# Moving the start addresses of TensorE's operands in SBUF, in a fused two-block transformer kernel

## The reference

```python
# block 1
h    = rmsnorm(x, g_attn)
proj = h @ w_in                       # 2048 x 6144, and 8 forget-gate columns
mixed = concat(head_rmsnorm(stick_breaking(q, k, v)), head_rmsnorm(forgetting(q, k, v, log_f)))
x    = x + mixed @ w_out              # 2048 x 2048
u    = relu(rmsnorm(x, g_mlp) @ w_up) # 2048 x 8192
x    = rmsnorm(x + (u * u) @ w_down, g_final)
# block 2
proj = rmsnorm(x) @ w_in_2            # 2048 x 7168, and 16 narrow columns
x    = x + concat(hgrn2(...), gated_delta(...)) @ w_out_2
x    = x + peer(rmsnorm(x))           # 16384 experts: all up products, top-16 gates, all down products
return rmsnorm(x, final_norm_g_2)
```

## Time and profile before

| | |
|---|---|
| time, median of 2 runs | 3211.09 us (3210.66 to 3211.52) |
| span of the profiled execution, first to last instruction | 3209.0 us |
| time less span | 2.1 us |
| mean granted TensorE clock | 0.999 |
| TensorE busy | 3191.6 us, 99% of the span, 19975 matmuls |
| VectorE, ScalarE, GpSimd busy | 2030.1, 1447.3, 496.9 us |
| DMA | 644.18 MB, mean 201 GB/s |

### The profile page before, as it was taken

How to read it: one execution, slowest core, us unless ns; L and a number is a source line. 1 busy time by engine, 2 the same in 40 slices (tenths; PEclk the granted TensorE clock), 3 DMA queues, 4 the chain that set the end, 5 groups by cost and what they waited for, 6 DMA issues and landing times.

```text
span 3209.0 us, 48201 instructions
## 1 busy us (share of the span) xinstructions
PE 3191.6 (99%) x19975; PEld 2854.0 (89%) x19975; DVE 2030.1 (63%) x1837; ACT 1447.3 (45%) x1271; POOL 496.9 (15%) x418
## 2 busy tenths in 40 slices
PE   9999999999999999999999999999999999999999
PEld 7888899999999888888989999999999888888887
DVE  5455665556555667765476888999975555555554
ACT  5454453333433364464444444555544433334333
POOL 0000000000000002136200002888840000000000
PEclk9999999999999999999999999999999999999999
DMA  7444565555555453342255566677676656556563
GB/s 282 165 159 158 172 225 194 196 186 193 195 187 193 158 183 119 132 158 105 93 211 204 199 216 222 224 251 251 229 263 259 241 225 261 228 230 257 226 261 118
DMA packets 129572, 644.18 MB, mean 201 GB/s; under 512 B 12672, under 2 KB 45840, under 8 KB 60304
## 3 DMA queue, kind: packets, MB, share of 16 engines
q1 hardware_dynamic: 95792, 623.03, 53.3%
q10 hardware_dynamic: 33632, 18.99, 1.9%
HBM read 606.31 MB, written 35.66 MB: 200 GB/s over the span
## 4 chain that ended last, share of the span: by engine, by line
PE 97%; DVE 1%; ACT 1%; DMA 0%; SPq 0%; issue 0%; DVEq 0%; ACTq 0%
PE pj L305 12%; PE pj L304 12%; PE pj L306 12%; PE pj L282 7%; PE pj L281 7%; PE pj L280 7%; PE pj L1774 4%; PE pj L1772 4%; PE pj L890 4%; PE pj L892 4%; PE pj L1773 4%; PE pj L891 4%; PE pm L282 2%; PE pt L282 2%; PE pt L281 2%; PE pm L281 2%
## 5 line engine op out<-in xcount | busy, mean ns | idle before, releaser
L262 ACT ACTIVATE hi<-raw 128x2048 fp32r<-128x2048 f32 x534 | 1023.8, 1917 | 1372.7 <-PE pj L306 640.7
L269 DVE TENSOR_TENSOR lo<-raw,hi 128x2048 fp32r<-128x2048 f32 x400 | 918.5, 2296 | 677.5 <-ACT hi L262 676.7
L304 PE MATMUL pj<-xh,hi 128*128 128x256 f32 x3328 | 919.9, 276 | 0.0
L305 PE MATMUL pj<-xl,hi 128*128 128x256 f32 x3328 | 918.8, 276 | 0.0
L306 PE MATMUL pj<-xh,lo 128*128 128x256 f32 x3328 | 918.8, 276 | 0.0
L305 PEld LDWEIGHTS pj<-xl,hi 128*128 128x128 f32 x3328 | 625.0, 188 | 0.6
L304 PEld LDWEIGHTS pj<-xh,hi 128*128 128x128 f32 x3328 | 624.8, 188 | 0.6
L306 PEld LDWEIGHTS pj<-xh,lo 128*128 128x128 f32 x3328 | 624.8, 188 | 0.0
L269 DVE TENSOR_TENSOR lo_in<-raw,hi 128x2048 fp32r<-128x2048 f32 x134 | 308.1, 2300 | 268.9 <-ACT hi L262 268.4
L2495 POOL TENSOR_SCALAR hotA<-cst,slotT 128x128 fp32r<-128x128 f32 x256 | 337.9, 1335 | 462.0 <-ACT slotT L2333 425.4
L1772 PE MATMUL pj<-hi,xh 128*128 128x512 f32 x576 | 232.3, 403 | 0.0
(11 more groups left out here) (408 smaller groups left out, 4243.8 us busy)
## 6 DMA issues: line engine op xcount, KB each, us to landing
raw<-w_peer SPq DMA_DIRECT2D x256, 1024.0 KB, 6.3
raw<-w_mlp SPq DMA_DIRECT2D x128, 1024.0 KB, 4.8
raw<-w_in SPq DMA_DIRECT2D x102, 1024.0 KB, 4.8
raw<-w_out SPq DMA_DIRECT2D x32, 1024.0 KB, 4.8
raw<-w_q SPq DMA_DIRECT2D x16, 1024.0 KB, 4.9
act_scratch<-hidU SPq DMA_DIRECT2D x32, 512.0 KB, 3.0
gates_scratch<-stage ACTq DMA_DIRECT2D x8, 2048.0 KB, 17.5
hidV<-act_scratch SPq DMA_DIRECT2D x32, 512.0 KB, 3.7
```

The lines of the kernel that those rows point to most:

```text
L262: nc.scalar.activation(hi[:, j, :], raw[:, j, :], ACT.Copy).then_inc(hi_ready, 1)
L269: nc.vector.tensor_tensor(low(q)[:, j, :], raw[:, j, :], hi[:, j, :].bitcast(F32), ALU.subtract).then_inc(lo_ready, 1)
L304: nc.tensor.matmul(o, hi[:, j, cols], xh[:, k0 + k, :], start=clears, stop=False, skip_group_check=True)
L305: nc.tensor.matmul(o, hi[:, j, cols], xl[:, k0 + k, :], start=False, stop=False, skip_group_check=True)
```

## The change

No instruction is added, removed or moved; operands begin elsewhere. Each slot of `hi` gets 8 elements (32 bytes) of padding, each slot of `lo` 12 elements (48 bytes); `xl` moves 64 bytes away from the end of `xh`; the four split coefficient buffers of the MLP and the four of the experts get a `rest` each.

```diff
+STEP, LO_STEP = 8, 12
...
-        hi = sb("hi", [P, SLOTS, CH], F32R)
+        hi = sb("hi", [P, SLOTS, CH + STEP], F32R)
         at_lo = cursor[0]
-        lo = sb("lo", [P, SLOTS, CH], F32R)
+        lo = sb("lo", [P, SLOTS, CH + LO_STEP], F32R)
...
         xh = sb("xh", [P, KT, TT * P], F32R)
+        cursor[0] += 64
         xl = sb("xl", [P, KT, TT * P], F32R)
...
-        coef_h = [y(f"coef_h{i}", [P, 4, TT * P], F32R) for i in range(2)]
-        coef_l = [y(f"coef_l{i}", [P, 4, TT * P], F32R) for i in range(2)]
+        coef_h = [y(f"coef_h{i}", [P, 4, TT * P], F32R, rest=128 * i) for i in range(2)]
+        coef_l = [y(f"coef_l{i}", [P, 4, TT * P], F32R, rest=128 * i) for i in range(2)]
...
-            nc.scalar.activation(hi[:, j, :], raw[:, j, :], ACT.Copy).then_inc(hi_ready, 1)
+            nc.scalar.activation(hi[:, j, 0:CH], raw[:, j, :], ACT.Copy).then_inc(hi_ready, 1)
...
-            nc.vector.tensor_tensor(low(q)[:, j, :], raw[:, j, :], hi[:, j, :].bitcast(F32),
+            nc.vector.tensor_tensor(low(q)[:, j, 0:CH], raw[:, j, :], hi[:, j, 0:CH].bitcast(F32),
                                     ALU.subtract).then_inc(lo_ready, 1)
...
-        cV_h = [y(f"cV_h{i}", [P, 4, TT * P], F32R) for i in range(2)]
-        cV_l = [y(f"cV_l{i}", [P, 4, TT * P], F32R) for i in range(2)]
+        cV_h = [y(f"cV_h{i}", [P, 4, TT * P], F32R, rest=256 + 128 * i) for i in range(2)]
+        cV_l = [y(f"cV_l{i}", [P, 4, TT * P], F32R, rest=256 + 128 * i) for i in range(2)]
```

## The result

The changed kernel takes 3277.59 us (median of 3277.41 to 3277.76) against 3211.09 us: a ratio of 1.0207, 95% interval 1.0178 to 1.0237. It is slower by 66.5 us, outside the range and 5 us from the rival "the new distances put the products into the slower pace". That it is slower is clear; whether by more than 2% is not, as the interval begins at 1.0178.

A forecast was written before the change was run, and what follows sets the result against it. TensorE's matmul count times the distance between starts was taken as the bound; all terms summed to 0, so profiled 3209.0 us plus 2.1 us for the median gave 3211 us, range 3105 to 3250 us.

The forecast's parts named there:

- the new distances put the products into the slower pace: Experts and MLP, where starts now coincide in places: all matmuls +72 us, 3283 us; chance 0.15, 0.10 of it beyond 2%.
- What bounds the kernel: TensorE, busy 3191.6 of 3209.0 us: time is number of matmuls times distance between starts; the change moves both operands' addresses.
- Makers: ScalarE writing `hi` and VectorE writing `lo` to padded slots: both have cover, costed at nothing.
- other engines: VectorE, ScalarE, GpSimd or DMA slowing TensorE's reads: the pace is TensorE's own, so removing contention is worth nothing.
- alignment: Slots 1 and 3 of `hi` and `lo` start off multiples of 64: taken as zero, upper bound +72 us.
- shifts of the rest: Moves of `resid`, `cst`, regions and DMA targets behind `xl`: work under TensorE's products, zero.
- TensorE's two streams against each other: Weight load beside the moving stream, starts 192 bytes apart before, 0 to 256 after: taken as zero, upper bound +72 us.
- (1): Transposes streaming `cst` past `proj1` (distance 192) and `resid` (distance 0): eight take 1.04 us in both cases, no effect.
- (2): Narrow products, stationary start stepping 128 bytes, claimed through all four distances: block 2 at 0.1132 us, block 1 at 0.1168 us.
- The faster rival: Distance 192 holds back the 512-column products: 106 us gained, 3105 us, chance 0.22; or a small gain, chance 0.13.
- the up products' relative pace: The small gain in 512-column products: 0.2267 us each, 15 us, 3196 us; chance 0.13.
- The rival that the change doesn't do what it says: Some operands still share remainders; if only fully distinct ones gain, again 3211 us; counted within the 0.50 for no effect.

The follow-up runs named there:

- the matmul kernel: Nothing but matmuls, against no other kernel: one operand distance per line, later one distance after another; 113.3 to 120.0 ns at 256 columns, no total time given.

## Why the prediction was wrong

**What bounds the kernel** was right: the loss is the number of matmuls times the change of their distance, with no wait in it. One sentence there says too much: not every matmul has two operands that the change moves. `lo_in` and slot 0 of `hi` stay in place, and with slot 2 of `hi` a part of the products keep 64 or 192. The distance changes in eleven matmuls of twelve.

**Makers, other engines, alignment, shifts of the rest**, each costed at nothing: right. Makers 1917 and 2294 ns; the pace of the matmul kernel, with every other engine idle, is that of the full one; the moving operand's own remainder made no difference at 512 columns (0, 32, 64, 128, 320), and none at 256 columns between 0 and 320, the two series that go through the same distances in the same order; moving everything behind `xh` by 256 bytes cost nothing.

**The step that failed** is in "TensorE's two streams against each other": "I take zero from (1) and from block 2 in (2), which is nearest: same engine state, same 256 columns, all distances." The measured value of that term is +67 us, near the upper end (+72) that stood beside it. The three rows failed in three ways.

- *Block 2's narrow products* were not "all distances". Their stationary start moves by 128 bytes a step from 192 by 512, past `xh` and `xl` at 320: with a period of 256, that is distance 0 and 128 and no third. Nor do they stand for the wide products: they load 32 and 16 columns, and in the matmul kernel 32 columns ran at 113.3 at distance 128 and, in one line of two, at distance 0. What these rows show is a fast state of another load, and of two distances. In the changed kernel, where the distances are 0, 64, 128 and 192, the same 32 matmuls are slower:

```profile
1192.38 0.28 PE L610 MATMUL pm<-xh,wtail_s 128*32 128x256 f32 x1
...
1196.01 0.28 PE L612 MATMUL pm<-xl,wtail_s 128*16 128x256 f32 x1
```

32 matmuls, 31 steps from start to start, in 3.63 us are 0.1171 us each, where it was 0.1132: the row that stood for "no effect" moved with the change itself.
- *The transposes* are plain float32 with 128 columns, and were no price for the 32-bit matmul format with 256: eight of them take 1.03 to 1.04 us in the changed kernel and in each of the three that moved slots, `xh` or `xl` alone, while the products around them changed pace.
- *Rows with the slower paces* were in hand: block 1's 0.1168 and 0.2333, near what the matmul kernel gives for a bad distance (116.7 to 120.0; 230 to 234). The prediction used them as the upper end only. But neither is the price of a distance of the wide products: block 1's load is narrow, and both chunks of the earlier trace rows stand at 192, so they show two paces at one distance, as the prediction half said ("unchanged addresses do not exclude it"). The up products of the kernel before have two as well. This is the first chunk of the MLP, at distance 64:

```profile
418.77 0.28 PE L304 MATMUL pj<-xh,hi 128*128 128x256 f32 x1
...
423.72 0.28 PE L304 MATMUL pj<-xh,hi 128*128 128x256 f32 x1
```

42 steps in 4.95 us are 0.1179 us each, against 0.1133 in the earlier trace rows. So the kernel before held no price for the wide products at the new distances, and zero was a choice, not a reading.

**The slower rival** was right in its first half, new distances and a slower pace. That its total is only 5 us off is in part luck, since two errors cancel. Up products: 3.5 ns taken, 4.7 measured (47.3 us in place of 35). Down products and projections: 4.7 ns taken, 2.1 to 3.0 measured (18.7 us in place of 37, since distances 0, 192 and 240 are among theirs). The 4.7 itself should have been 4.4: 0.2286 is a rounding of the earlier trace rows, all starts of down products give 228.9. Its reason "stationary and moving now coincide" is right for up products (0.1200 at distance 0) and the reverse of the truth for down products, which are at their fastest there. It wanted nine matmuls in ten at its prices for the 2%. Every group of the table above lost, but the up products more than priced, the others about half.

**The faster rival** asked whether 192 holds the 512-column products back. It does, by 228.9 - 226.7 = 2.2 ns, not by the 13.6 ns of the plain float32 product: no distance of the 32 went below 226.7, which is twice 113.3. Its small case, "the up products' relative pace" with 15 us, named that floor exactly. The change did not get it, because it gave distance 0 to a part of the down products only, and took 64 away from the up products, which carry 9984 matmuls.

**The rival that the change doesn't do what it says** fell on its premise: distinct remainders gain nothing by themselves. Remainders 256 apart run like equal ones (L5256 and L5000, 0.1197 us both), and slots at 128 and 384 by turns gave 3210.68 us. A kernel in which all operands are distinct was not run.

What is shown: while one distance lasts, the pace follows it by 256, through the load of the stationary operand, with no other engine; and at one and the same distance the matmuls before decide between two paces (113.3 and 117.8 at 256 columns and 64; 226.7 and 233.3 at 512 columns and 16). What is not: what inside the chip makes either, what pace a mixture of distances gets, and by what rule the matmuls before decide (512 columns at 128 left a fast pace in the full kernel and a slow one in the matmul kernel). Not tried: projections at distance 0 with the up products left at 64. Both use `xh` at one address, and the run that moved it gained 4.5 us in the projections and lost 65.4 in the up products.

## What to carry to other kernels

When TensorE is busy without a gap, the start addresses of its two operands are part of the tiling: measure the distance from start to start at several distances of the operands, in a kernel of matmuls alone and with the full width of the stationary operand, and in the mixture and order of the kernel itself, before any buffer is moved or padded. Fix the distance for each product by its own columns (here 64 for 256 columns, 0 for 512, by remainder of 256), and look at the products that run next, since they may carry on the pace of those before. A row that shows no effect is a price only if it has the same operand type, the same load and distances that differ by the right period; where a row beside it shows an effect, zero is not the reading.

## What the runs showed of the hardware that was not expected

- Two reads of one engine disturb each other. The Trainium skill ("SBUF — State Buffer", section "Who interferes with whom") has them as two independent read ports, and by that rule the sum of the change would be zero. The full kernel lost 66.5 us and the matmul kernel shows 113.3 to 120.0 ns at 256 columns with all other engines idle; the measurement decides. The rule's other half, that TensorE waits on no other engine, agrees with the windows of the kernel before (709 and 708 matmuls with GpSimd busy for 71.48 and 0 us) and of the one with two remainders by turns (708 and 708).
- The Trainium skill ("TensorE: Matmul & The Clock Gate", section "Wait — 56ns, not 53.3ns?") gives 2.5 ns over the columns at 2.4 GHz, which would be, as an estimate, 215.8 ns for 512 columns and 109.2 for 256. In this 32-bit format the best of 32 distances gave 226.7 and 113.3, with the clock granted in full: an excess of 13 and 7 ns over the columns.
- The same matmuls at the same addresses have two paces, 113.3 and 117.8 ns, and keep either for as long as the product lasts: 96 matmuls in the matmul kernel, 192 in the MLP's blocks. Products of 512 columns have two as well: 226.7 and 233.3 ns at distance 16 in the matmul kernel, 0.2289 and 0.2333 us at 192 in the kernel before.
